# Rounding the step-size weights on VectorE and scaling the fourth tile of x on GpSimd

## The reference

```python
def rmsnorm(x, g):
    xf = x.astype(jnp.float32)
    y = xf * lax.rsqrt(jnp.mean(xf * xf, axis=-1, keepdims=True) + EPS)
    return (y * g.astype(jnp.float32)).astype(x.dtype)

def hybrid_layer(x, pre_norm_g, w_in, ...):
    b, L, _ = x.shape
    h = rmsnorm(x, pre_norm_g)
    proj = h @ w_in
    q, k, v, z_attn, z_ssm, xbc, dt_raw = jnp.split(proj, cuts, axis=-1)
    ...
```

## Time and profile before

| | us |
|---|---|
| runs: median (lowest to highest), 3 runs | 2406.3 (2404.64 to 2406.3) |
| the profiled execution, its time | 2405.06 |
| the profiled execution, its span | 2403.3 |
| PE busy | 2381.7 (99%) |
| DVE busy | 1810.1 (75%) |
| ACT busy | 1007.8 (42%) |
| POOL busy | 473.0 (20%) |
| granted TensorE clock, mean | 0.998 of 2.4 GHz |

### The profile page before, as it was taken

The page is one execution under the profiler, slowest core; times in us unless marked ns, Lnnn a source line. Parts: engine busy times, 40 slices in busy tenths (PEclk is TensorE's granted clock), DMA queues, the critical chain, the costliest instruction groups (busy, mean ns, idle before and its releaser), DMA issues.

```text
span 2403.3 us, 36544 instructions
## 1 busy us (share of the span) xinstructions
PE 2381.7 (99%) x13556; PEld 2263.0 (94%) x13556; DVE 1810.1 (75%) x2608; ACT 1007.8 (42%) x1685; POOL 473.0 (20%) x764
## 2 busy tenths in 40 slices
PE   7999999999999999999999999999999999999998
PEld 7999999999999999999999999999999988888887
DVE  5686766666666577777776799999999868787767
ACT  6323433333333333333333555565565533334332
POOL 0000177777775011111110001001000000000000
PEclk9999999999999999999999999999999999999999
DMA  5234466666666344444444666666675535445544
GB/s 165 78 105 158 142 195 205 206 203 208 207 203 185 99 140 141 138 144 138 138 138 160 227 199 198 190 189 202 197 217 165 177 127 176 158 156 130 175 166 158
DMA packets 322390, 402.70 MB, mean 168 GB/s; under 512 B 23478, under 2 KB 242934, under 8 KB 319847
## 3 DMA queue, kind: packets, MB, share of 16 engines
q1 hardware_dynamic: 266551, 226.78, 31.1%
q0 software_dynamic: 30352, 97.98, 13.5%
q10 hardware_dynamic: 25376, 76.53, 9.2%
HBM read 310.99 MB, written 97.56 MB: 170 GB/s over the span
## 4 chain that ended last, share of the span: by engine, by line
PE 98%; DVE 1%; DMA 1%; ACT 0%; issue 0%; SPq 0%; DVEq 0%
PE ps L1180 44%; PE ps L1343 14%; PE ps L1047 14%; PE ps L928 8%; PE ps L1267 5%; PE ps L1148 2%; PE ps L1104 2%; PE ps L1067 2%; PE ps L1085 1%; PE ps L1159 1%; PE ps L950 1%; PE ps L1131 0%; PE ps L878 0%; PE ps L1110 0%; PE ps L1075 0%; PE ps L964 0%
## 5 line engine op out<-in xcount | busy, mean ns | idle before, releaser
L1180 PE MATMUL ps<-h_hi,w_hi 128*128 128x384 f32 x1152 | 386.7, 336 | 0.0
L1180 PE MATMUL ps<-h_lo,w_hi 128*128 128x384 f32 x1152 | 386.4, 335 | 0.0
L1180 PE MATMUL ps<-h_hi,w_lo 128*128 128x384 f32 x1152 | 386.0, 335 | 0.0
L2468 DVE TENSOR_TENSOR w_lo<-raw_qk,w_hi 128x512 fp32r<-128x512 f32 x288 | 226.6, 787 | 156.2 <-ACT w_hi L1704 154.8
L1180 PE MATMUL ps<-t_hi,w_lo 128*128 128x384 f32 x864 | 292.2, 338 | 0.0
L1180 PE MATMUL ps<-t_hi,w_hi 128*128 128x384 f32 x864 | 291.9, 338 | 0.1
L1180 PE MATMUL ps<-t_lo,w_hi 128*128 128x384 f32 x864 | 291.1, 337 | 0.0
L1704 ACT ACTIVATE w_hi<-raw_qk 128x512 fp32r<-128x512 f32 x288 | 181.2, 630 | 257.0 <-PE ps L1180 257.0
L1180 PEld LDWEIGHTS ps<-h_lo,w_hi 128*128 128x128 f32 x1152 | 216.4, 188 | 0.0
L1180 PEld LDWEIGHTS ps<-h_hi,w_lo 128*128 128x128 f32 x1152 | 216.2, 188 | 0.0
L1180 PEld LDWEIGHTS ps<-h_hi,w_hi 128*128 128x128 f32 x1152 | 216.2, 188 | 0.0
(11 more groups left out here) (369 smaller groups left out, 5282.2 us busy)
## 6 DMA issues: line engine op xcount, KB each, us to landing
raw_qk<-in_w_in SPq DMA_DIRECT2D x108, 512.0 KB, 4.5
w_raw<-in_w_in SPq DMA_DIRECT2D x128, 256.0 KB, 3.7
stage<-loc_scr ACTq DMA_DIRECT2D x32, 768.0 KB, 5.1
stage<-t_scr SPq DMA_DIRECT2D x48, 512.0 KB, 3.8
stage<-in_w_in SPq DMA_DIRECT2D x36, 512.0 KB, 5.2
stage<-in_w_out SPq DMA_DIRECT2D x36, 512.0 KB, 3.7
stage<-zx_scr ACTq DMA_DIRECT2D x46, 384.0 KB, 9.2
zx_scr<-w_raw SPq DMA_DIRECT2D x36, 384.0 KB, 3.3
```

Source lines behind the costliest of these rows:

```text
L1180: ins = nc.tensor.matmul(ps[:, bank, 0:HALF_T], w, h(k), start=(start and kk == 0 and q == 0), stop=(last and kk == KC - 1 and q == 2), sk ...
L2468: nc.vector.tensor_tensor(w_lo[:, n_slot(n, pp), :], src, w_hi[:, n_slot(n, pp), :].bitcast(f32), ALU.subtract).then_inc(w_lo_done, 1)
```

## The change

The rounding of the four chunks of step-size weights moves from ACT to DVE, where it stands right before the difference that reads it, with the wait for the chunk's DMA. The scaling of tile 3 of x (the fourth tile) moves from DVE to POOL, as POOL's first instruction behind a wait for the reciprocal, with a semaphore of its own. The mean and the reciprocal of that tile stay on DVE. TensorE waits for POOL's semaphore for tile 3, and its counts for tiles 4 and 5 are one lower.

```diff
+POOL_ROWS = 3
...
         x_squared, x_ms, x_root, x_rinv, x_scaled = (sem(n) for n in (
             "x_squared", "x_ms", "x_root", "x_rinv", "x_scaled"))
+        x_scaled_pool = sem("x_scaled_pool")
...
@@ the queue of POOL
+            t = POOL_ROWS
+            pool.wait_ge(x_rinv, t + 1)
+            nc.gpsimd.tensor_scalar(x_rows[t], x_rows[t], rx[:, t:t + 1], None, ALU.mult).then_inc(x_scaled_pool, 1)
+
             pool.wait_ge(cb_stored, 16 * SSM_GROUPS)
             pool.wait_ge(half_done, HP)
             load_first(0)
...
@@ the queue of TensorE
                     if half == 1 and k == 0:
-                        pe.wait_ge(x_scaled, t + 1)
+                        if t == POOL_ROWS:
+                            pe.wait_ge(x_scaled_pool, 1)
+                        else:
+                            pe.wait_ge(x_scaled, t)
...
@@ the queue of ACT, in its loop over turns
                                      scale=pre_cols[:, k:k + 1]).then_inc(h_hi_done, 1)
-                if n in W_TURNS:
-                    c = W_TURNS[n]
-                    act.wait_ge(w_in_s[c], 16)
-                    nc.scalar.activation(dt_cols(w_hi, c), dt_cols(w_raw, c), ACT.Copy).then_inc(w_hi_done, 1)
...
@@ the queue of DVE, scale_x and the loop over turns
                 dve.wait_ge(x_rinv, t + 1)
-                nc.vector.tensor_scalar(x_rows[t], x_rows[t], rx[:, t:t + 1], None, ALU.mult).then_inc(x_scaled, 1)
+                if t != POOL_ROWS:
+                    nc.vector.tensor_scalar(x_rows[t], x_rows[t], rx[:, t:t + 1], None, ALU.mult).then_inc(x_scaled, 1)
...
                 if n in W_TURNS:
                     c = W_TURNS[n]
+                    dve.wait_ge(w_in_s[c], 16)
+                    copy(dt_cols(w_hi, c), dt_cols(w_raw, c)).then_inc(w_hi_done, 1)
                     dve.wait_ge(w_hi_done, c + 1)
                     nc.vector.tensor_tensor(dt_cols(w_lo, c), dt_cols(w_raw, c), dt_cols(w_hi, c).bitcast(f32),
                                             ALU.subtract).then_inc(w_lo_done, 1)
```

## The result

Twenty runs of each kernel gave a median of 2409.88 us (2406.77 to 2410.95) against 2405.6 us (2403.18 to 2406.81) for the kernel before. The ratio is 1.0016, 95% interval 1.001 to 1.0022: slower by 2.4 to 5.3 us. The medians differ by 4.3 us, less than the 4.8 us that the prediction took as what can be told from no change, and the median lies 0.6 us above the range's upper end of 2409.3.

What follows compares the result with a forecast made beforehand. PE, 99% busy, bounds the kernel, so delays before 31 us count fully. Copies +0.77 and hold +0.38 make +1.15 us: 2406.2 from the profiled 2405.06, 2407.4 from the median 2406.3, middle 2406.8; range 2404.6 to 2409.3.

Steps and rivals of the forecast that it cites:

- What bounds it; one to one to the end: PE is busy 99%; a delay before 31 us, at turn 17 (30.16), reaches the end one to one.
- Removed from ACT and DVE: nothing but 0.31: Only the rounding before the square of tile 5 counts, -0.31 us on ACT's branch; DVE's 1.20 us scaling becomes idle time.
- Added to DVE: four copies at 0.39, +0.77 in all: Copies before the differences, 0.35 us plus 0.04 waiting each, make turn 11 late by +0.77 us (+0.59 to +0.98).
- POOL's start at 20.42: POOL begins scaling tile 3 once the reciprocal is there, at 20.42 us.
- POOL's duration, 2.6 us: POOL's scaling of tile 3 was estimated at 2.6 us, until 23.0, from half of the additions' 6.0.
- 5 us or more: Sign of being wrong: POOL's instruction scaling tile 3 takes 5 us or more.
- row bound from above: Upper bound for POOL's scaling of tile 3: eight times its 0.75 us addition of 128x256, 6.0 us.
- What POOL does to DVE: the hold, D - 2.2: POOL's scaling of D us stops chunk 2's copy, costing D - 2.2 us, +0.38 forecast, nothing below 2.2.
- a longer hold: Rival: POOL's scaling needs 3.4 to 6.2 us; at D = 5 the sum is 3.6, 2408.7 us; chance 0.17.
- If only the difference were held, the term would be 0: If POOL stopped chunk 2's difference but not its copy, the +0.38 us hold would be 0.
- The rules of the Trainium skill: DVE's two-SBUF-input or two-port instructions and POOL's SBUF reads exclude each other; one-input POOL work near line-rate, about 1.7 us.
- The number: Whole kernel: +1.15 us, forecast 2406.8 us, range 2404.6 to 2409.3, no change within 0.2%.

Runs made afterwards that it cites:

- e1: Changed kernel with tile 3 scaled by DVE as before, rounding still on DVE; median 2405.71 us against 2405.08 for the kernel before.
- f2: Changed kernel with the split of chunk 2 beside turn 4 instead of 5; trace alone, turns 16 to 18 run from 34.26 us.
- f3: Changed kernel with POOL scaling 1024 of tile 3's 2048 columns, the others left unscaled; median 2405.94 us against 2406.18 for the kernel before.
- g2: Changed kernel with chunk 2's split beside turn 4 and POOL's scaling replaced by a memset of 2700 columns; trace alone, turn 17 at 31.12 us.
- e2: Kernel before with only tile 3's scaling moved to POOL, rounding left on ACT; median 2405.9 us against 2405.08 for the kernel before.
- g1: Changed kernel with splits beside turns 1, 2, 3 and 12, so no copy or difference falls into POOL's instruction; median 2407.06 us.
- f1: Kernel before with tile 3's scaling on POOL and chunk 2's split beside turn 4; trace alone, difference ended 3.99 us after POOL's start.

## Why the prediction was wrong, step by step

- *What bounds it; one to one to the end.* Right. The shift at turn 17, 3.63, was 3.65 at the milestone, 50 us later, and 3.6 between the groups of runs.
- *Removed from ACT and DVE: nothing but 0.31.* Right. DVE had 1.14 us of idle before turn 5 instead of 0.27: the scaling's 1.20 us went there, less the copies, as the text had it. ACT's branch gained its 0.31 (the square of tile 5 came 3.41 us late, the mean of tile 4 3.72), but DVE's branch was the later one, 3.65, as forecast.
- *Added to DVE: four copies at 0.39, +0.77 in all.* Right in place, a little too dear: 0.28 and 0.03 of waiting, 0.31 each. Alone (e1) they cost 0.6 where the text had 0.77.
- *POOL's start at 20.42.* 20.34.
- *POOL's duration, 2.6 us.* This is the step that failed. It took 5.44 us, and 5.44 or 5.45 in all five kernels that scale the whole tile in one instruction, whatever DVE did beside it. The text had named 5 us or more as a sign of being wrong. The estimate halved the rate of the additions because one input is read instead of two. The runs give 1.56, 2.85 and 5.44 us for 512, 1024 and 2048 columns, so 0.26 us and 2.53 ns a column; an addition of 256 columns took 0.75, which is 1.9 ns a column if its start costs the same 0.26 us. By that estimate the one-input scaling is not cheaper a column than the two-input addition. The row bound from above, 6.0 us, was near; I should have taken the value at its side.
- *What POOL does to DVE: the hold, D - 2.2.* The mechanism was right: copy of chunk 2, from 22.6 to the end of POOL. With D = 5.44 the text's own formula gives 0.77 + 3.24 = 4.0. Measured were 3.63: the hold was 3.09 (3.37 less 0.28), and the other 0.54 are three copies at 0.31 less the 0.39 us that h_lo of turn 8 had had to spare. That is the rival named a longer hold, which the text gave 0.17 and priced at +3.6 for D = 5. What the text had of it from the earlier trace rows was thin, one pair, and in it the difference had begun 0.25 us before POOL's addition; for the copy the text had no row at all, only the rule that it names. The runs (e1, f2, f3, g2) show it.
- *If only the difference were held, the term would be 0.* Not at D = 5.44: e2 shows a hold of 1.04 us for the difference alone. At D = 2.6 no run tried it.
- *The rules of the Trainium skill.* The Trainium skill (SBUF — State Buffer, Who interferes with whom) was borne out in who holds whom: h_lo with its bank in PSUM kept 0.62 us inside POOL's instruction, the difference and the copy didn't, a write-only POOL instruction held the copy alone. It says that the second fully blocks until the first finishes; here that holds for the copy, while a difference was let go at 3.6 of 5.45 us. The one-input rate that the Trainium skill (GPSIMD Engine Reference, Engine selection) calls roughly line-rate was not seen: 5.44 us where that would be about 1.7, an estimate with that page's 1.2 GHz and one column a cycle.
- *The number.* The upper end, 2409.3, took in half of the longer hold. From the median of before, 2405.6, a shift of 3.6 is 2409.2, just inside it; the measured 2409.88 has 0.7 more from the shares of the groups 1.6 us apart, a spread that my three runs hardly showed. So the hold, sized from 2.6 us, put the forecast of 2406.8 too low, and it was the groups that took the median over the end of the range.

## What to carry to other kernels

Before work is handed to GpSimd, list the VectorE instructions that fall into its span. Here those with SBUF on both sides (copies, scalings) stood still until about its end, and the chain behind them, mean, root, square, next h_hi, stood with them. Price GpSimd's instruction by its own rows and by its row bound from above, since its length set the hold. And in a stage in which two engines alternate, idle time lies ahead of one instruction and not ahead of the next: moving a small mean and the splits (two tables) gave 0.9 us in the trace, where moving 1.2 us of work off VectorE gave nothing.

## What the runs showed of the hardware that was not expected

- A scaling of one float32 tile on GpSimd took 2.53 ns a column (0.26 us a start), a memset of 2700 columns 2.35 us in all, 0.87 ns a column.
- GpSimd's one instruction let VectorE's two kinds go at two points: differences of two SBUF tiles 3.6 us after its start, copies and a scaling only about at its end at 5.45.
- After the wait of 2.73 us before 27.04 PE was granted half its clock from 27 to 30 us. Waits of about 2.1 us went both ways: in g1 the clock was at half from about 29 to 32, in f1 it stayed full.

```profile
27.00:30.00 3.00, 2.96 (x11) 2.63 (x12) 2.73 (x6) 3.00 (x5) 0.00 (x0) 0.50 0.41 104
```

In the changed kernel this cost nothing more, since PE had to wait for DVE again at 33.26. Where the wait was 3.51 us (f2), the milestone product came at 87.06, 0.52 us after the changed kernel's, and DVE's h_lo of turn 11 was 0.53 later too (33.65 against 33.12): no share of the clock's own is seen there either.
